# A two-block transformer kernel on one core: two row norms merged, the context normalised in the layer's tail, and a loop of two layers written out

## The chip, the cores and the metric

The kernel runs on one core of one Trainium2 chip. The metric is the device time of one execution, in microseconds. The kernel before took 1733.14 us, the median of three runs (1732.53 to 1736.98).

## The reference

Two blocks run one after the other on x, 256 tokens of 1024 values. The first is two hybrid attention layers, each `x + merged(x) @ w_out`, and a norm over each token's 1024 values. The second block takes the result and a context `ctx` of 256 tokens. Its first step is again a norm of both, followed by a gain, a scale and a shift.

```python
def rms_norm(x, gain):
    y = x * lax.rsqrt(jnp.mean(x * x, axis=-1, keepdims=True) + RMS_EPS)
    return y * gain

def first_block(...):
    for layer in range(DEPTH):                 # DEPTH = 2
        h = hybrid_layer(h, norm_gain[layer], w_in[layer], ..., w_out[layer])
    return rms_norm(h, final_gain)

def modulate(x, g, shift, scale):
    return rms_norm_2(x, g) * (1 + scale) + shift

def second_block(x, c, ctx, ...):
    # layer 0: even mixer, layer 1: attention, each followed by a convolved feed-forward
    h = modulate(x, norm1_g[0], sh1, sc1)
    h_c = modulate(ctx, norm1_g[0], csh1, csc1)
    ... even_mixer(h), even_mixer(h_c): p = h @ w_in; parts f, u, v of p ...
```

## The kernel before

All tensors are held transposed, 1024 values as KC = 8 chunks of 128 partitions with the tokens along the free dimension; `x_t` is x and `c_t` the context. A product is done in three matmuls on split operands: `w_hi` is the weight rounded to fp32r by ScalarE (`high(u)`, L1242 in the layers and L1398 behind them), `w_lo` the rest, by VectorE (`low(u)`, L1753 and L2025). The activations are split in the same way (`o_hi`/`o_lo`, `h2_hi`/`h2_lo`).

A unit is one load of 1 MB of weights into one of four slots of `raw` and the matmuls on them, into one or two of the three banks `banks_g` (a job each). `high` and `low` of a unit run two units ahead (AHEAD = 2), and SP loads a slot when the unit four before is done. A layer is the list `ORDER` of 48 units with what lies between them; `ada` entries are 24 small products for the second block's scales and shifts, each with a load of 1 MB of its own. Every engine walks the same list and emits its part of each entry; so the order on an engine is the order of the list, and semaphores counted by name (`Steps`) tie the engines together. Before the change each engine runs the layer as a hardware loop, `Fori(0, DEPTH)`, and values that depend on the layer sit in registers.

The layer's tail is units 44 to 47 (`out` 0 to 3). VectorE adds each product to `x_t` (L1812). ScalarE then rounds x times the next gain into `o_hi` (L1300, "x gain") and squares it into `qk[0]` (L1203), and VectorE makes `o_lo` (`x_low`, L1713) and adds the squares (L1708). In units 46 and 47 `high(0)`, `high(1)` and `first_low(0)`, `first_low(1)` (L1720) split the weights of the next pass, or of the units `vs` behind the last pass; `first_low` stands ahead of the addition of that unit's product. The layer ends with `ada turn` 1 on TensorE (L818), `mod now` on VectorE (L2004) and its copy to `mod` (L2017).

Behind the layers the list `END` sets the order. It begins with the final norm: sums of the squares over the partitions by matmuls with a column of ones (L712), a square root on ScalarE (L1519), a reciprocal (L2127), a spread of the 256 values over all partitions by a matmul (L1065) and eight multiplications into `x_t` (L2133). Then come transposes of the context (L1044), copies to `c_t` (L1497), squares of x and context (L1512), their additions (L2121), sums (L1059), root, spread (L1065) and the modulated norm in eight chunks: `h2` on VectorE for chunks 0 and 1 (L2142) and on GpSimd for the others (L1692), scale and shift on ScalarE (L1538), a cast and a subtraction on VectorE (L2149, L2152). Units `vs` 0 and 1 (L996 and L1020), of four 128-token tiles each, take these chunks; `sgu weights` transposes w_s (L1072), and unit `f` follows (L1032). `c_in` (the context as loaded) is issued on SP behind the last load of the layer (L657), and four constants are issued from ScalarE's queue (L1402 to L1405).

Of the kernel before, what the change touches and what calls it, by code (L numbers as in the profile page):

```python
# [50 lines left out]
SUM_COL = 352  # L51
# [60 lines left out]
class Steps:  # L112
# [13 lines left out]
    def step(self, *names):  # L126
        self.count[self.part] += 1
        for name in names:
            self.names[(self.part, name)] = self.count[self.part]
        return 1  # L130

# [61 lines left out]
def layer_order():  # L193
# [8 lines left out]
    for n, (kind, i) in enumerate(layer_units()):  # L202
# [39 lines left out]
        if n >= 44:  # L242
# [3 lines left out]
            order.append(("sums", n - 44))  # L246
        if n == 47:
            order.append(("ada turn", 1))
# [19 lines left out]
def end_order():  # L268

    order = [("final norm",), ("ctx",)]  # L270

    def all_squares(tag):
        order.extend(("squares", tag, c) for c in range(KC))
        order.extend(("sums", tag, c) for c in range(KC))
# [24 lines left out]
    all_squares("00")  # L299
    order.append(("mod norm", 0, 0))  # L300
    units("vs", 2)
# [45 lines left out]
END_UNITS = [(kind, i) for what, *rest in END if what == "unit" for kind, i in [rest]]  # L347
# [8 lines left out]
for _kind, _i in END_UNITS:  # L356
    for _j in range(end_jobs(_kind)):
        END_JOBS[(_kind, _i, _j)] = len(END_JOBS)
# [19 lines left out]
def program(nc, ins, out, known):  # L378
    with ExitStack() as ctx:
# [74 lines left out]
        add_parts = sb("add_parts", [P, 2 * PACK])  # L454
        token_rstd1 = sb("token_rstd1", [P, 2])
# [12 lines left out]
        s_cols = sb("s_cols", [P, KC, S_AT + 32])  # L468
# [54 lines left out]
        c_in = sb("c_in", [P, 2, D], offset=probs_at)  # L523
        used2 = max(used2, area + 16384 + 256)
        assert used2 <= SBUF_BYTES, used2
# [21 lines left out]
        end_loaded = sem("end_loaded")  # L547
        odd_loaded = sem("odd_loaded")
# [30 lines left out]
        def norm_tiles(tag):  # L579

            return 2 if tag in ("f", "11") else 4
# [23 lines left out]
        def _(sp):  # L605
# [4 lines left out]
            with sp.Fori(0, DEPTH) as layer:  # L610
                enter("layer", layer)
                w_in_l = ins["w_in"][bass.ds(layer, 1)].rearrange("l (c p) n -> (l p) c n", p=P)
# [5 lines left out]
                for u, (kind, i) in enumerate(UNITS):  # L618
# [5 lines left out]
                    if kind == "branch":  # L624
                        n, half = divmod(i, 2)
                        src = ins["w_branch"][bass.ds(layer, 1), n].rearrange("l (c p) n -> (l p) c n", p=P)[
                            :, :, half * 512:half * 512 + 512]
                        dst = slot.rearrange("p (c n) -> p c n", c=4)
                    else:
                        dst = slot.rearrange("p (c n) -> p c n", c=KC)  # L630
                        if kind == "out":
                            src = ins["w_out"][bass.ds(layer, 1)].rearrange("l (c p) n -> (l p) c n", p=P)[
# [8 lines left out]
                    sp.dma_start(dst, src).then_inc(raw_loaded[u % SLOTS], 16)  # L641
                    if u == 1:
# [3 lines left out]
                    if u and u % 2 == 0 or u == len(UNITS) - 1:  # L646
# [5 lines left out]
                                     ins["ada_w"][bass.ds(layer, 1)].rearrange("l (c p) n -> (l p) c n", p=P)[  # L652
# [3 lines left out]
            sp.wait_ge(pe_steps, pe_.at("values15"))  # L656
# [1618 lines left out]
```

## Time and profile before

| | |
|---|---|
| median of three runs | 1733.14 us |
| profiled execution, its own time | 1733.48 us |
| its span | 1731.7 us |
| PE busy / weight loads | 1637.4 us (95%) / 1431.8 us (83%) |
| VectorE (DVE) busy | 994.4 us (57%) |
| ScalarE (ACT) busy | 734.1 us (42%) |
| GpSimd (POOL) busy | 97.1 us (6%) |
| mean granted clock of TensorE | 0.971 |
| read from HBM | 256.67 MB |

PE is TensorE. Its matmuls overlap in the records, so that busy time is not time at its peak, and the distance between the starts of two matmuls tells more than their length. A granted clock of 1.0 is 2.4 GHz and one of 0.5 is 1.2 GHz. In a row of the timeline, the time in square brackets is how long the engine had been idle, and behind the arrow stands what ended it; a wait for several things is put down to the one that came last.

### The profile page before, as it was taken

How to read it: one execution, taken by the hardware profiler on the slowest of the kernel's cores; microseconds unless marked ns; L12 is line 12 of the kernel's file. 1: busy time of each engine (PE TensorE's matmuls, PEld its weight loads, DVE VectorE, ACT ScalarE, POOL GpSimd, SP SyncE). 2: the span in 40 equal slices, each digit the busy share in tenths (PEclk: the TensorE clock that was granted, in tenths of full speed). 3: DMA queues.
4: the chain of work that ended last, by engine and by line, in shares of the span. 5: the costliest groups of instructions: out<-in, count | busy, mean ns of one | idle time of the engine just before them, and what ended most of it. 6: DMA issues, size and time to landing. Idle time of an engine off the chain costs nothing.

```text
span 1731.7 us, 29254 instructions
## 1 busy us (share of the span) xinstructions
PE 1637.4 (95%) x11791; PEld 1431.8 (83%) x11791; DVE 994.4 (57%) x1243; ACT 734.1 (42%) x1072; POOL 97.1 (6%) x71
## 2 busy tenths in 40 slices
PE   6999999999999999779989999999979999989998
PEld 6998998989989989668777888888868785789998
DVE  6888566568885665563346433444344315677674
ACT  4545544445545444353235322233234233755453
POOL 0110000002100000020002000000011101210000
PEclk9999999999999999879999999999988998999999
DMA  7775665766766667602032223322233422145764
GB/s 253 232 251 175 219 218 192 249 209 215 244 197 217 195 196 240 220 25 98 25 97 70 85 67 108 115 86 78 87 110 101 125 73 61 38 147 172 206 180 125
DMA packets 329967, 259.68 MB, mean 150 GB/s; under 512 B 24017, under 2 KB 322385, under 8 KB 329826
## 3 DMA queue, kind: packets, MB, share of 16 engines
q1 hardware_dynamic: 311184, 251.55, 45.7%
q10 hardware_dynamic: 18642, 6.19, 1.7%
q8 instruction: 96, 1.57, 0.4%
q14 instruction: 45, 0.37, 0.1%
HBM read 256.67 MB, written 1.05 MB: 149 GB/s over the span
## 4 chain that ended last, share of the span: by engine, by line
PE 73%; DVE 14%; ACT 7%; issue 3%; DMA 2%; POOL 1%; ACTq 0%; SPq 0%; DVEq 0%
PE banks_g L1032 33%; PE banks_g L779 18%; PE banks_g L769 4%; PE banks_g L1020 3%; DVE w_lo L2025 3%; ACT w_hi L1398 3%; PE banks_g L802 2%; DVE w_lo L1753 2%; ACT w_hi L1242 1%; DVE conv L2074 1%; PE bank_s L899 1%; PE bank_t L912 1%; POOL h L1692 1%; DMA raw<-w_in 1%; DVE h_lo L2152 1%
## 5 line engine op out<-in xcount | busy, mean ns | idle before, releaser
L1032 PE MATMUL banks_g<-h_hi,w_lo 128*128 128x512 f32 (+1 forms) x864 | 297.7, 345 | 9.7 <-DVE h_lo L2152 9.7
L2025 DVE TENSOR_TENSOR w_lo<-raw,w_hi 128x2048 fp32r<-128x2048 f32 (+1 forms) x100 | 208.0, 2080 | 156.4 <-ACT w_hi L1398 156.4
L1032 PE MATMUL banks_g<-h_lo,w_hi 128*128 128x512 f32 (+1 forms) x864 | 295.8, 342 | 0.0
L1032 PE MATMUL banks_g<-h_hi,w_hi 128*128 128x512 f32 (+1 forms) x864 | 295.7, 342 | 0.0
L1753 DVE TENSOR_TENSOR w_lo<-raw,w_hi 128x2048 fp32r<-128x2048 f32 x92 | 210.7, 2290 | 82.1 <-ACT w_hi L1242 81.8
L779 PE MATMUL banks_g<-h_hi,w_lo 128*128 128x256 f32 x800 | 228.0, 285 | 0.0
L779 PE MATMUL banks_g<-h_lo,w_hi 128*128 128x256 f32 x800 | 223.4, 279 | 0.0
L779 PE MATMUL banks_g<-h_hi,w_hi 128*128 128x256 f32 x800 | 223.4, 279 | 0.0
L1398 ACT ACTIVATE w_hi<-raw 128x2048 fp32r<-128x2048 f32 (+1 forms) x100 | 173.3, 1735 | 73.6 <-DMA raw<-w_down 47.1
L1032 PEld LDWEIGHTS banks_g<-h_hi,w_lo 128*128 128x128 f32 x864 | 164.0, 190 | 33.3 <-DVE h_lo L2152 12.0
L1242 ACT ACTIVATE w_hi<-raw 128x2048 fp32r<-128x2048 f32 x96 | 182.9, 1905 | 7.4 <-DMA raw<-even_in 3.5
L1032 PEld LDWEIGHTS banks_g<-h_hi,w_hi 128*128 128x128 f32 x864 | 164.3, 190 | 21.0
L1032 PEld LDWEIGHTS banks_g<-h_lo,w_hi 128*128 128x128 f32 x864 | 164.3, 190 | 20.9
L1032 PE MATMUL banks_g<-f_hi,w_lo 128*128 128x512 f32 (+1 forms) x480 | 161.9, 337 | 3.0 <-DVE f_lo L2043 1.5
L1032 PE MATMUL banks_g<-f_hi,w_hi 128*128 128x512 f32 (+1 forms) x480 | 161.5, 336 | 0.0
L1032 PE MATMUL banks_g<-f_lo,w_hi 128*128 128x512 f32 (+1 forms) x480 | 161.5, 336 | 0.0
L779 PEld LDWEIGHTS banks_g<-h_hi,w_lo 128*128 128x128 f32 x800 | 151.1, 189 | 8.3 <-issue 5.0
L779 PEld LDWEIGHTS banks_g<-h_hi,w_hi 128*128 128x128 f32 x800 | 150.9, 189 | 0.0
L779 PEld LDWEIGHTS banks_g<-h_lo,w_hi 128*128 128x128 f32 x800 | 150.7, 188 | 0.0
L779 PE MATMUL banks_g<-o_hi,w_lo 128*128 128x256 f32 x480 | 135.4, 282 | 0.0
L779 PE MATMUL banks_g<-o_lo,w_hi 128*128 128x256 f32 x480 | 133.3, 278 | 0.0
L779 PE MATMUL banks_g<-o_hi,w_hi 128*128 128x256 f32 x480 | 133.3, 278 | 0.0
(322 smaller groups left out, 2882.8 us busy)
## 6 DMA issues: line engine op xcount, KB each, us to landing
raw<-w_in SPq DMA_DIRECT2D x76, 1024.0 KB, 5.1
ada_raw<-ada_w SPq DMA_DIRECT2D x48, 1024.0 KB, 7.3
raw<-w_up SPq DMA_DIRECT2D x88, 512.0 KB, 4.6
raw<-w_down SPq DMA_DIRECT2D x32, 704.0 KB, 4.4
raw<-w_branch SPq DMA_DIRECT2D x12, 1024.0 KB, 5.1
raw<-qkv SPq DMA_DIRECT2D x12, 1024.0 KB, 4.9
raw<-w_out SPq DMA_DIRECT2D x8, 1024.0 KB, 5.0
raw<-even_in SPq DMA_DIRECT2D x6, 1024.0 KB, 5.4
```

Source lines behind the costliest of these rows:

```text
L769: last = nc.tensor.matmul(ov[:, t, :], a[:, c, t * P:t * P + P], w[:, c, :], start=c == 0 and n == 0, stop=c == KC - 1 and n == 2)
L779: last = nc.tensor.matmul(ov[:, m, :], w[:, c, m0:m0 + P], a[:, a0 + c, :], start=c == 0 and n == 0, stop=c == kcs - 1 and n == 2)
L802: last = nc.tensor.matmul(gb[r, 0:256], s_cols[:, c, s0:s0 + 32], aw[:, c, :], start=c < 4, stop=c >= 4)
L899: last = nc.tensor.matmul(bank_s[:, 2 * e + j, 0:nk], qs[r, c, qt * P:qt * P + P], keys, start=x != "c", stop=True)
L912: last = nc.tensor.transpose(bank_t[:, s, :], probs[k % 2][:, s, kt * P:kt * P + P], ident[:, :])
L1020: last = nc.tensor.matmul(gb[:, tt * 256:tt * 256 + 256], a[:, c, t0:t0 + P], w[:, c, :], start=c == 0 and n == 0, stop=c == KC - 1 and n ...
L1032: last = nc.tensor.matmul(gb[:, m * SEQ:m * SEQ + nt], w[:, c, m0:m0 + P], a[:, c, 0:nt], start=c == 0 and n == 0, stop=c == kcs - 1 and n ...
L1242: nc.scalar.activation(w_hi[:, u % SLOTS, :], raw[:, u % SLOTS, :], ACT.Copy).then_inc(act_steps, act_.step(f"hi{u}"))
L1398: nc.scalar.activation(w_hi[:, u % SLOTS, 0:n], raw[:, u % SLOTS, 0:n], ACT.Copy).then_inc(act_steps, act_.step(f"hi{u}"))
L1692: nc.gpsimd.tensor_tensor(h2[:, c, t], x_streams[s_][:, c, :], m_rstd[:, t], ALU.mult).then_inc(pool_steps, pool_.step(f"normed{tag} {c}"))
L1753: nc.vector.tensor_tensor(w_lo[:, u % SLOTS, :], raw[:, u % SLOTS, :], w_hi[:, u % SLOTS, :].bitcast(F32), ALU.subtract).then_inc(dve_step ...
L2025: nc.vector.tensor_tensor(w_lo[:, u % SLOTS, 0:n], raw[:, u % SLOTS, 0:n], w_hi[:, u % SLOTS, 0:n].bitcast(F32), ALU.subtract).then_inc(dv ...
```

## The change

The two passes of the layer are written out for every engine: `Fori` becomes a Python loop, and `again()` sets the count of the steps back for each pass. `first_low(0)` and `first_low(1)` on VectorE, and `high(0)` and `high(1)` on ScalarE, move behind the additions and squares of units 46 and 47. The sums of the squares at the layer's start go to `bank_o` and no longer wait for `mod now`; the product `small` does.

In the second pass alone: SP issues the context and the four constants behind the weights of unit 42. The tail makes squares of x (qk[0]) and of x times the final gain (`y_sq`), no `o_hi` and no `o_lo`. "ctx prep" squares the rows of the context as loaded, with the sum along the row (tokens on partitions), takes their root and reciprocal, and scales the rows into `c_n`.

Behind the layers, the context comes first: `c_n` is transposed, gets gain and shift (ctx h), is split, and feeds the context half of `vs` 0. Both norms of x are got from one set of sums: r1 = 1/sqrt(sum x²/D + eps), r2 = 1/sqrt(r1² · sum (x·gain)²/D + eps); r1 and r1·r2 are spread together. h2 of x is one multiplication by both gains (`fg_gain`) and r1·r2; the shift goes into the rounding, and no work is left for GpSimd in this norm. `vs` is taken in four parts: 0 context, 1 context, 0 x, 1 x. The copies of the context into `c_t` and the final norm of `x_t` itself ("x prime") stand behind them. The diff, cut to its core:

```diff
@@ def end_order()
-    order = [("final norm",), ("ctx",)]
+    order = [("ctx turn", b) for b in range(4)] + [("final sums",)]
+    order += [("ctx h", 0), ("ctx h", 1), ("ctx split", 0), ("ctx h", 2), ("final root",), ("ctx h", 3), ("ctx split", 1),
+              ("second root",), ("ctx h", 4), ("ctx h", 5), ("ctx split", 2), ("ctx h", 6), ("ctx h", 7),
+              ("ctx split", 3)]
...
-    all_squares("00")
-    order.append(("mod norm", 0, 0))
-    units("vs", 2)
+    order += [("part", "vs", 0, 1), ("spread00",), ("x norm", 0)]
+    for c in range(1, KC):
+        order += [("x norm", c), ("x split", c - 1)]
+    order += [("x split", KC - 1), ("part", "vs", 1, 1), ("part", "vs", 0, 0), ("ahead", 2), ("part", "vs", 1, 0),
+              ("ahead", 3), ("ctx",), ("x prime",)]
@@ each engine
-            with pe.Fori(0, DEPTH) as layer:
+            for layer in range(DEPTH):
                 enter("layer", layer)
+                pe_.again()
@@ SP, in the layer
+                    if u == 42 and layer == DEPTH - 1:
+                        sp.dma_start(c_in[:, :, :], ins["ctx"][0].rearrange("(t p) f -> p t f", p=P)
+                                     ).then_inc(ctx_loaded, 16)
+                        sp.dma_start(dft_c[:, :], ins["dft_c"]).then_inc(end_loaded, 16)
+                        sp.dma_start(dft_t[:, :, :, :], ins["dft_t"]).then_inc(end_loaded, 16)
...
@@ ACT, in the layer
-                        high((u + AHEAD) % len(UNITS))
+                        if u + AHEAD < len(UNITS):
+                            high(u + AHEAD)
...
                         squares(i)
+                        if i >= 2:
+                            high(i - 2)
...
+                    elif what == "ctx prep" and layer == DEPTH - 1:
...
+                            for t in range(2):
+                                nc.scalar.activation(c_n[:, t, :], c_in[:, t, :], ACT.Square,
+                                                     accum_out=token_root[:, 2 + t:3 + t]).then_inc(ctx_ready, 1)
...
+                            nc.scalar.activation(c_n[:, t, :], c_in[:, t, :], ACT.Copy,
+                                                 scale=token_rstd[:, 2 + t:3 + t]).then_inc(ctx_ready, 1)
@@ DVE, in the layer
                         if u + AHEAD < len(UNITS):
                             low(u + AHEAD)
-                        else:
-                            first_low(u + AHEAD - len(UNITS))
...
+                        if i >= 2:
+                            first_low(i - 2)
@@ PE, behind the layers
+                elif what == "final sums":
+                    pe.wait_ge(dve_steps, dve_.at("gated15", before=True))
+                    pe.wait_ge(x_squared, 10)
+                    pe.wait_ge(act_steps, act_.at("squares3", before=True))
+                    for n, parts in ((2, [y_sq[:, a, j, :] for a in range(2) for j in range(2)]),
+                                     (0, [qk[0][:, j, :] for j in (0, 1, 6, 7)])):
+                        for t in range(2):
+                            for j in range(4):
+                                last = nc.tensor.matmul(bank_o[:, SUM_COL + n + t:SUM_COL + n + t + 1],
+                                                        parts[j][:, t * P:t * P + P], ones[:, 0:1],
+                                                        start=j == 0, stop=j == 3)
...
                 elif what == "ctx":
                     pe.wait_ge(ctx_loaded, 16)
+                    pe.wait_ge(act_steps, act_.at(f"ctx h{KC - 1}"))
@@ DVE, behind the layers
+                elif what == "ctx split":
+                    b, = arg
+                    if b == 0:
+                        dve.wait_ge(pe_steps, pe_.at("final sums"))
...
+                elif what == "x norm":
...
+                    nc.vector.scalar_tensor_tensor(h2[:, c, 0:SEQ], x_t[:, c, :], fg_gain[:, c:c + 1],
+                                                   bank_m[:, SEQ:2 * SEQ], ALU.mult, ALU.mult
+                                                   ).then_inc(dve_steps, dve_.step(f"x norm{c}"))
+                elif what == "x split":
...
+                    nc.vector.scalar_tensor_tensor(h2_lo[:, c, 0:SEQ], h2[:, c, 0:SEQ],
+                                                   mod[:, 0, mod_col(0) + c, 0:1], h2_hi[:, c, 0:SEQ].bitcast(F32),
+                                                   ALU.add, ALU.subtract).then_inc(dve_steps, dve_.step(f"x split{c}"))
```

## Rows read from the trace of the kernel before

**Rows 1.** The page: shares of the chain, and the two weight splits (busy, mean ns).
```profile
PE 73%; DVE 14%; ACT 7%; issue 3%; DMA 2%; POOL 1%; ACTq 0%; SPq 0%; DVEq 0%
...
L1753 DVE TENSOR_TENSOR w_lo<-raw,w_hi 128x2048 fp32r<-128x2048 f32 x92 | 210.7, 2290 | 82.1 <-ACT w_hi L1242 81.8
...
L1242 ACT ACTIVATE w_hi<-raw 128x2048 fp32r<-128x2048 f32 x96 | 182.9, 1905 | 7.4 <-DMA raw<-even_in 3.5
```

**Rows 2.** Windows: length, busy of PE, PEld, DVE, ACT, POOL; clock; DMA share; GB/s.
```profile
367.60:721.60 354.00, 342.75 (x3126) 315.70 (x3126) 248.59 (x319) 166.09 (x252) 17.45 (x6) 0.99 0.66 216
721.60:728.60 7.00, 0.00 (x0) 0.00 (x0) 5.28 (x7) 3.11 (x4) 0.00 (x0) 0.71 0.43 150
728.60:754.10 25.50, 10.07 (x44) 9.40 (x45) 11.32 (x25) 11.52 (x28) 0.77 (x1) 0.57 0.12 37
```

**Rows 3.** PE's waits, 300 to 782 us: total, times, longest.
```profile
PE bank_m L1059 <- DVE h L2121: 7.7, 1, 7.7
PE bank_m L712 <- DVE mod_now L2004: 7.1, 1, 7.1
```

**Rows 4.** The chain in order of time: start, us, what.
```profile
371.15 8.23 PE banks_g L761 x48
...
769.50 11.31 PE banks_g L1020 x96
...
781.24 22.42 PE banks_g L1032 x96
```

**Rows 5.** Timeline of PE at both layers' ends: start, us, instruction, idle before.
```profile
371.15 0.58 PE L761 MATMUL banks_g<-o_hi,w_lo 128*128 128x256 f32 x1 [3.56 <-DVE x_t L1812]
...
721.07 0.52 PE L818 MATMUL bank_m<-add_parts,ada_sum 128*128 128x24 f32 x4
```

**Rows 6.** Timeline of DVE between the layers.
```profile
370.35 0.68 DVE L1812 TENSOR_TENSOR x_t<-banks_g,x_t 128x512 f32<-128x512 f32 x1
...
376.74 0.17 DVE L1759 COPY gain<-vec 128x8 f32 x1 [2.95 <-issue]
```

**Rows 7.** Timeline of DVE at the end of the second layer.
```profile
723.31 2.29 DVE L1720 TENSOR_TENSOR w_lo<-raw,w_hi 128x2048 fp32r<-128x2048 f32 x1 [1.01 <-ACT w_hi L1242]
```

**Rows 8.** Timelines of DVE and ACT: durations of operations that the change reuses.
```profile
720.59 0.88 DVE L1713 SCALAR_TENSOR_TENSOR o_lo<-x_t,gain_next,o_hi 128x256 fp32r<-128x256 f32 x2
...
735.67 3.22 DVE L2133 SCALAR_TENSOR_TENSOR x_t<-x_t,vec,bank_m 128x256 f32<-128x256 f32 x8 [1.32 <-PE bank_m L1065]
...
752.80 0.43 DVE L2149 CAST h_hi<-h 128x512 fp32r<-128x512 f32 x1 [0.50 <-ACT h L1538]
753.26 0.69 DVE L2152 TENSOR_TENSOR h_lo<-h,h_hi 128x512 fp32r<-128x512 f32 x1
...
732.59 1.28 ACT L1519 ACT_TABLE_LOAD   x1 [4.93 <-issue]
```

**Rows 9.** Timelines of SP and PE in the second layer; landings of c_in and ada_raw.
```profile
664.11 0.37 SPq L641 DMA_DIRECT2D raw<-w_branch  x1
...
676.31 1.07 PE L802 MATMUL banks_g<-ada_raw,s_cols 128*32 128x256 f32 x16
...
714.50 1.07 PE L802 MATMUL banks_g<-ada_raw,s_cols 128*32 128x256 f32 x16
...
DMA to landing us min/median/max: 7.2/7.2/7.2
...
DMA to landing us min/median/max: 5.1/7.9/7.9
```

**Rows 10.** Timeline of PE: the sums of squares at either level of the clock.
```profile
380.31 1.05 PE L712 MATMUL bank_m<-ones,qk 128*128 128x1 f32 x8
...
728.65 1.87 PE L712 MATMUL bank_m<-ones,qk 128*128 128x1 f32 x8 [7.06 <-DVE mod_now L2004]
```

**Rows 11.** DMA view, instruction packets: 17 to 368 us, then 368 to 722 us.
```profile
q8 instruction: 25, 0.41, 0.4%
...
q8 instruction: 27, 0.44, 0.5%
```

More of the change, by code:

```diff
@@ L50 @@
 ADA_COL = 256
-SUM_COL = 352
+SUM_COL = 384
 ADA_UNITS = 24
@@ L130, in step, with again @@
         return 1
+    def again(self):
+        self.count["layer"] = 0
     def total(self, part):
@@ L246, in layer_order @@
             order.append(("sums", n - 44))
+        if 43 <= n <= 46:
+            order.append(("ctx prep", n - 43))
         if n == 47:
@@ L346 @@
 END = end_order()
-END_UNITS = [(kind, i) for what, *rest in END if what == "unit" for kind, i in [rest]]
+END_UNITS = list(dict.fromkeys((rest[0], rest[1]) for what, *rest in END if what in ("unit", "part")))
+END_U = {name: u for u, name in enumerate(END_UNITS)}
 def end_jobs(kind):
@@ L355 @@
 END_JOBS = {}
-for _kind, _i in END_UNITS:
-    for _j in range(end_jobs(_kind)):
-        END_JOBS[(_kind, _i, _j)] = len(END_JOBS)
+for _what, *_rest in END:
+    if _what == "unit":
+        for _j in range(end_jobs(_rest[0])):
+            END_JOBS[(*_rest, _j)] = len(END_JOBS)
+    elif _what == "part":
+        END_JOBS[tuple(_rest)] = len(END_JOBS)
 END_JOB_AT = {n: job for job, n in END_JOBS.items()}
@@ L703, in _, with sum_squares @@
                 last.then_inc(pe_steps, pe_.step(f"x turned{b}"))
[L705 to L709 removed]
+            def sum_squares(layer):
+                pe.wait_ge(dve_steps, dve_.at("gated15", before=True))
+                pe.wait_ge(x_squared, layer * 3 + 3)
                 for t in range(2):
                     for j in range(2):
[L712 removed]
+                        last = nc.tensor.matmul(bank_o[:, SUM_COL + t:SUM_COL + t + 1],
                                                 qk[0][:, j, t * P:t * P + P], ones[:, 0:1],
@@ L833, in _ @@
                     elif what == "small":
-                        pe.wait_ge(act_steps, act_.at("root"))
                         pe.wait_ge(dve_steps, dve_.at("small lo"))
+                        pe.wait_ge(dve_steps, dve_.at("mod now", before=True))
                         n = 0
@@ L1230, in _ @@
                                      ).then_inc(act_steps, act_.step("s cols"))
-            with act.Fori(0, DEPTH) as layer:
+            for layer in range(DEPTH):
                 enter("layer", layer)
+                act_.again()
                 def high(u):
@@ L1650, in _ @@
             pool.wait_ge(consts_loaded, 16 * CONSTS)
-            with pool.Fori(0, DEPTH) as layer:
+            for layer in range(DEPTH):
                 enter("layer", layer)
+                pool_.again()
                 before = "rope r"
@@ L1744, in _ @@
             dve.wait_ge(consts_loaded, 16 * CONSTS)
-            with dve.Fori(0, DEPTH) as layer:
+            for layer in range(DEPTH):
                 enter("layer", layer)
+                dve_.again()
                 def low(u):
@@ L2016, in _ @@
                 own()
-                nc.vector.tensor_copy(mod[:, bass.ds(layer, 1), :, :], mod_now[:, :, :]
+                nc.vector.tensor_copy(mod[:, layer:layer + 1, :, :], mod_now[:, :, :]
                                       ).then_inc(dve_steps, dve_.step("mod"))
@@ L2122, in _ @@
                             dve_steps, dve_.step(f"added{tag} {c}"))
-                elif what in ("final norm", "mod norm"):
-                    tag = "f" if what == "final norm" else f"{arg[0]}{arg[1]}"
+                elif what == "mod norm":
+                    tag = f"{arg[0]}{arg[1]}"
                     tiles = norm_tiles(tag)
```

331 lines of the change are left out of this document (216 added, 115 removed).

## Prediction

> **What bounds the kernel now.** I began with the page: the chain of work that ended last is 73% PE, and a split of one 2048-wide weight unit costs 1.9 us on ACT and then 2.29 on DVE [rows 1]. A change counts for what it takes out of PE's waits. The windows come next [rows 2]: in the second layer PE is busy for 342.75 of 354.00 us; in the 32.5 us from 721.6 to 754.1 it is busy for 10.07 us in all, at a granted clock of 0.57 to 0.71, and that on sums, spreads and transposes only. The list of waits names the holes in that stretch [rows 3]: 7.1 us for mod_now, which stands in DVE's queue behind the last w_lo split (L1720, from 723.31) and the last addition to x (about 725.5, though its product was ready at 721.07) [rows 7], and 7.7 us for the additions of the squares. The chain gives the pace and the end of the stretch [rows 4]: 96 matmuls in 11.31 us, 0.118 us each, and unit f starts at 781.24. The layer's last matmuls (L818, 721.07 and 0.52 long [rows 5]) end at 721.6. Between the two lie 59.6 us that hold 192 matmuls of vs, 22.6 us at that pace. So some 37 us are at stake, less what the norms really need.
>
> A second hole lies between the layers: PE starts unit 0 at 371.15 after 3.56 us of idle time [rows 5], so it was free at 367.6. The granted clock is at its lower level, 1.2 GHz, after these 3.56 us without work, and the 48 matmuls take 8.23 us [rows 4] in place of 48 x 0.118 = 5.65.
>
> **Part 1, between the layers.** Two edits meet here: the loops are written out, and first_low (2.29 us) moves behind the additions to x. What ends the 3.56 us is ambiguous: the row names x_t (L1812, 370.35 to 371.03), which stood behind a first_low; but DVE itself has 2.95 us of "issue" idle before the first instruction of the next pass [rows 6], where nothing keeps it waiting, so the jump back costs time of its own. Both are removed. The new order: unit 47 and ada 23 (1.07 [rows 9]) take PE's last 6.7 us, so the product of unit 46 is there at 360.4 and is now added at once; hi(0) follows squares(2) on ACT and ends at about 364.6, first_low(0) at 366.9, before PE is free at 367.6. The last addition runs 367.1 to 367.8, x hi 6 and 7 to 368.7, x_low (0.44 each [rows 8]) to 369.3; unit 0 needs them for its last 12 matmuls, from 371.8. High(1) ends at 371.2, first_low(1) at 373.5; unit 1 comes behind unit 0 (367.6 + 5.65 = 373.2), ada 0 and sumsq (1.07 and 1.05), at 375.3. No wait is left and the clock stays up. Unit 0 ends at 373.2 for 379.4: **6.2 us** saved, 3.6 of the gap and 2.6 of the clock. The ends: 0 if PE must pay a fetch there in a straight run too; the same 6.2 if only x_t was late.
>
> Of fetching, the DMA view shows 25 packets of instructions during the first pass and 27 during the second [rows 11]: the second pass is fetched again already, and written out it fetches nothing more. The Trainium skill (Runtime: NRT & Kernel Launch, Instruction fetch mechanics) says that prefetch is purely sequential and that a taken branch out of the resident pages stalls; DVE's 2.95 us agree with it.
>
> **Part 2, the loads moved into the layer.** SP issues ctx (1 MB) and four constants (0.9 MB) behind unit 42's weights, at 664.11. Queued behind them on SP and on the DMA engines: ada 20, then the weights of units 43 and 44. An ada alone lands 5.1 us after its issue; c_in, 0.6 us behind another, took 7.2 and an ada just behind unit weights 7.9 [rows 9]: each further MB adds 2.7 to 3.8 us. So unit 42 lands at 669.2, the 1.9 MB at about 674.6, ada 20 at 677.4 to 678.3; PE wants ada 20 at 676.31. I take **+1.5 us** (0 to +3). The weights of 43 land at about 681, their split takes 4.2 us, and unit 43 is wanted about two units of PE behind ada 20: hidden. In return four issues in ACT's queue ahead of the final root go; that is inside part 4's new order.
>
> **Part 3, the tail of the second layer.** Added to ACT: two squares and two scaled copies of 128x1024, 1.0 each (half of 1.9), a table load of 1.28 [rows 8], a root of 0.3; to DVE three operations of 0.2 and two additions of 0.69. The x hi copies become squares, x_low goes. Behind them on ACT stand the weight splits: high(46) ends at 702.8 for 700.9; high(47) at 710.9, behind the root; low(47) at 713.2, needed by unit 47 at 715.5 (ada 23 at 714.50 and 1.07 [rows 9]). Behind low(47) on DVE, the addition that frees out1's bank ends at 713.9, also needed at 715.5. So all is hidden, with 1.6 us to spare. The Trainium skill (ScalarE: Activation LUTs, What ACT_TABLE_LOAD costs) adds a drain of 1.38 us to a load; this trace shows the root 0.02 us behind the load. By the page the slack would shrink to 0.2 us and the sum stay.
>
> Then out2's addition ends 717.6, x hi 718.5, squares 719.1, high(0) 721.0, the last context copy 722.0; first_low(0) 723.3, out3's addition 724.0, its squares 725.5, high(1) 727.4, first_low(1) 729.7, mod 730.3.
>
> **Part 4, behind the layer.** PE: twelve context transposes from 722.1, four more at 724.0, from 725.5 the final sums, 16 matmuls of one column where there were 4. Four took 1.05 us at 2.4 GHz and 1.87 at 1.2 [rows 10]: 16 are 4.2 or 7.5 us. Before, the clock was down at 728.65, after 7 us idle; here PE works 1.8 of 4 us. I take the lower level, since such light work did not raise it before either (0.57 from 728.6 to 754.1 [rows 2]): sums to 733.0, other end 729.7. [...]
>
> DVE's first context split waits for the sums: cast 0.43, subtraction 0.69 [rows 8], their forms without POOL at work: 734.2; the small steps of the root 734.9; splits 1 to 3, with r12 between them, 736.0, 737.6, 738.8. PE takes the first 48 matmuls (vs 0, context) from 734.2, with the clock down at first, as unit 0 did: 8.2 us, 742.4, longer than the splits. Spread, 4 matmuls: 743.5. Then vs 1, context, 5.65: 749.1. Beside it x is made: product 0.40 [rows 8], split 0.45, some 0.87 a chunk, from 743.9 to 751.3. PE takes up x at 749.1, 0.71 a chunk, chunk 7 at 754.1: no wait. vs 0 ends 754.8, vs 1 760.4, sixteen transposes 762.3.
>
> **The new wait:** on ACT stand, in this order, the gelu of the last vs (761.0), high(3) 1.9 (762.9) and only then four 128x512 copies of c_t, 0.5 each (764.9); the transposes of w_s wait for the last. PE idles 2.6 us, and f starts at 765.6. Behind that, x prime (8 x 0.40, after low(3), to 768.4) holds low(4) to 770.7, needed two units on: hidden. Saved up to f: 781.24 - 765.6 = **15.6 us**.
>
> **Sum**, against the profiled execution's own 1733.48 us (1.8 above its span; the median is 1733.14): 1733.5 - 6.2 + 1.5 - 15.6 = 1713.2. Behind f order, loads and bound are the old ones.
>
> **Rivals.**
> - The clock stays up through the sums: PE's gaps there are short. They end 3.3 us earlier: 1709.9; if it stays up into vs too, 2.6 more, 1707.3. Chance 0.20.
> - More waits: the pause before f drops the clock too (2.6 us, as unit 0 paid), or ada 20 and out1's bank come later: 1716. Chance 0.17.
> - Part 1 doesn't do what it says, PE pays a fetch there anyway: 1713.2 + 6.2 = 1719.4. Against: no wait of that size on "issue" among PE's [rows 3]. Chance 0.09.
> - Slower than before: written out, PE's stream outruns its fetch when the DMA engines are loaded (share 0.66 in the layer [rows 2]). A miss priced like the 3.56 us gap must come six times to eat 20 us; ten of the 27 fetches would give 1713.2 + 35.6 = 1748.8. Against: the end part is straight already and its PE shows none. Chance 0.02.
> - Within 0.3%: parts 1 and 4 both lose most of their gain (order kept, clock down to f): about 1730. Chance 0.02.
>
> **How the numbers follow.** Forecast 0.50, at 1713.2. The 80% range takes in the bounds of ada 20 (-1.5, +1.5) and the cases beside it, and leaves out the failure of part 1: 1707 to 1719. The bound for same, 0.3% or 5.2 us, is about what a measurement of this kernel can tell from no change: faster 0.96, same 0.02, slower 0.02.
>
> **What would show it.** PE's gap between the layers gone and unit 0 at 5.65 us; ada 20 waited for by 1 to 2 us; final sums of some 7 us; unit f about 20 us earlier; a new PE wait of 2 to 3 us for c_t ahead of it. It is wrong if PE waits for the splits of x, if low(47) or out1's bank stalls PE before 721, or if stages behind f change length.

## Result and the profile after

The changed kernel takes 1723.05 us (median of six runs, 1716.71 to 1725.65) beside 1734.45 for the kernel before: ratio 0.9929, 95% interval 0.9911 to 0.9947. It is faster by 11.4 us where 20 were forecast; 1723 lies 4 us above the top of the range. A second measurement, beside later experiments, gave 1721.12 and 0.9922 (0.9908 to 0.9936). The profiled executions, 1719.86 against 1733.48, are 13.6 us apart, and the account below is made between those two; the one of the changed kernel is the second fastest of its six.

The windows of PE in the kernel after come first (length, busy time of PE, PEld, DVE, ACT and POOL with their counts, granted clock, DMA share, GB/s). The last one runs from the end of the layer's last product to the start of unit f:

```profile
0.00:369.90 369.90, 347.19 (x3146) 319.77 (x3147) 256.71 (x332) 174.81 (x266) 19.18 (x15) 0.99 0.68 224
369.90:724.40 354.50, 343.57 (x3143) 315.93 (x3143) 248.05 (x320) 174.23 (x263) 18.40 (x6) 1.00 0.67 220
720.70:762.40 41.70, 36.08 (x270) 35.34 (x270) 21.13 (x37) 20.72 (x34) 0.00 (x0) 0.88 0.22 77
```

The same stretch in the kernel before, which holds the two last windows of [rows 2] and the matmuls of vs behind them:

```profile
721.60:781.24 59.64, 36.33 (x241) 34.94 (x242) 33.57 (x48) 28.30 (x51) 12.01 (x12) 0.74 0.16 51
```

PE is busy for 36 us in both; the stretch has shrunk from 59.6 to 41.7 us. The two long waits of [rows 3] are gone. What PE waits for in the whole run now (total, times, longest):

```profile
PE bank_t L941 <- DVE probs L1887: 13.9, 10, 2.3
PE bank_t L1137 <- DVE token_rstd L2304: 5.7, 3, 1.9
PE bank_t L1144 <- ACT c_t L1613: 2.8, 1, 2.8
...
PE banks_g L832 <- DMA ada_raw<-ada_w: 0.8, 1, 0.8
```

and what answered to the first two in the kernel before:

```profile
PE bank_t L912 <- DVE probs L1775: 11.2, 10, 1.7
PE bank_t L1065 <- DVE token_rstd L2127: 2.3, 4, 0.6
```

Ten waits for probs have grown by 2.7 us in all, though the attention of the layers is not among the things that the change names; and three waits for token_rstd cost 5.7 us where four cost 2.3.

Where the time went shows best in the same piece of PE's work in both traces, each timed from its own first instruction. The shift is the start after less the start before (negative is earlier), at anchors that both kernels have:

| place in PE's stream | start before | start after | shift |
|---|---|---|---|
| first unit | 17.36 | 17.43 | +0.1 |
| an ada product late in layer 0 | 334.41 | 336.57 | +2.2 |
| ada 0 of layer 1, behind unit 0 | 379.31 | 375.59 | -3.7 |
| last probs of layer 1 | 643.66 | 641.95 | -1.7 |
| ada 22 of layer 1 | 702.00 | 701.13 | -0.9 |
| transposes of w_s, just ahead of unit f | 780.64 | 761.75 | -18.9 |
| spread of the norm "01" | 905.25 | 887.73 | -17.5 |
| spread of the norm "10" | 1288.29 | 1272.99 | -15.3 |
| first up unit of the last FFN | 1539.77 | 1525.68 | -14.1 |
| last down units | 1633.04 | 1619.63 | -13.4 |

So the boundary gave 5.9 and the tail 18.0; the layers took 2.1 and 2.9 back, and the stages behind unit f took 5.5 (each is the difference of two shifts, before rounding). The chain of the kernel after through the tail, in order of time (start, length, what), shows no long piece in which PE idles:

```profile
724.42 5.00 PE bank_o L1024 x32
...
729.44 0.44 DVE h_hi L2192
...
729.90 0.69 DVE h_lo L2194
730.60 0.09 DVE token_r L2199
...
730.74 8.62 PE banks_g L999 x48
739.36 0.89 PE bank_m L1034 x8
740.25 16.98 PE banks_g L999 x144
...
757.28 0.47 issue
757.75 1.90 ACT w_hi L1497
759.65 1.96 ACT c_t L1613 x4
...
761.75 0.63 PE bank_t L1144 x4
```

Three things stand in it: the sums take 5.0 us, unit vs 0's context half is slow (8.6, as unit 0 once was in [rows 4]) and the other 144 matmuls of vs run at full pace without a gap, and then ACT's split of 1.90 stands ahead of the copies of c_t.

### The profile page after: what moved, and what is told of

Read it like the earlier page. It is cut to its first block, busy times and chain, and to the rows that moved or that the text cites. A ratio compares the mean times of both kernels' runs of the same rounds, so it can differ in the third digit from the quotient of the medians.

```text
span 1718.0 us, 27660 instructions
## 1 busy us (share of the span) xinstructions
PE 1637.9 (95%) x11819; PEld 1431.4 (83%) x11819; DVE 980.7 (57%) x1238; ACT 731.2 (43%) x1062; POOL 86.6 (5%) x59
## 4 chain that ended last, share of the span: by engine, by line
PE 55%; DVE 12%; ACT 6%; issue 2%; DMA 1%; POOL 1%; SPq 0%; DVEq 0%; ACTq 0%
PE banks_g L1109 33%; PE banks_g L809 6%; DVE w_lo L2154 3%; PE banks_g L1097 3%; ACT w_hi L1497 3%; DVE w_lo L1865 2%; PE banks_g L999 1%; DVE conv L2252 1%; ACT w_hi L1315 1%; POOL h L1803 1%; PE bank_t L1165 1%; PE banks_g L1079 1%; PE banks_g L799 1%; PE banks_g L832 1%; PE bank_m L1189 1%
```

## Experiments

Every ratio is to the kernel before, on the same chip, with its 95% interval. Two questions were open: what the layers pay, and what the norms behind x prime pay. A third was which of two edits closed the gap between the layers.

### The boundary: jump or order

One kernel writes the loops out and leaves the order:

```diff
-            with dve.Fori(0, DEPTH) as layer:
+            for layer in range(DEPTH):
+                dve_.again()
```

(and so for the other four engines). 

> The kernel before with its five loops over the layers written out and nothing else changed. Theory A: writing out costs each layer 2 to 3 us (waits that were register compares become instructions of their own on DVE's chains: PE's waits for probs at 2.3, 2.0, 0.9 and 1.8 us for 1.7, 1.6, 0.5 and 1.3). At the boundary between the layers, if the jump was the cause, the gap of 3.56 us goes and the clock stays up (6.2 us gained): net about -1 us against before. If x_t, late behind first_low, was the cause, the gap stays above 3 us and the net is +4 to +5. Rival B, the prediction's: the layers cost nothing by being written out and only the boundary changes: -3 to -6 us. Rival C, a straight stream is fetched late: the layers grow with waits on issue, not with longer waits for probs.

The other keeps the loops and moves only the splits:

```diff
 (ACT, squares i)
+                        if i >= 2:
+                            high(i - 2)
 (DVE, sums i)
+                        if i >= 2:
+                            first_low(i - 2)
```

(and takes them out of units 46 and 47, as the change does).

> The kernel before with its loops kept; only the first two weight splits of the next layer (high 0 and 1 on ACT, first_low 0 and 1 on DVE) are moved behind the squares and sums of out3, as the change has them. If x_t late behind first_low made the 3.56 us gap between the layers, the gap goes: -6 us against before, and the tail of the second layer is untouched. If the jump back made it (DVE showed 2.95 us of issue there), some 3 us of gap stay, the clock still falls, and the time is within 1 us of before. Both layers should keep their old lengths otherwise (waits for probs 1.7, 1.6, 0.5, 1.3).

Measured: loops written out 1733.09, ratio 0.9989 (0.9977 to 1.0); order alone 1734.71, ratio 0.9989 (0.9979 to 1.0). Timelines of PE at the start of unit 0, first the loops written out, with the row ahead of it, then the order alone:

```profile
370.94 0.52 PE L823 MATMUL bank_m<-add_parts,ada_sum 128*128 128x24 f32 x4
371.30 0.36 PE L766 MATMUL banks_g<-o_hi,w_lo 128*128 128x256 f32 x1
```

```profile
371.98 0.58 PE L761 MATMUL banks_g<-o_hi,w_lo 128*128 128x256 f32 x1 [4.42 <-issue]
```

Written out, PE goes on without a gap although first_low still stands where it stood. With the order alone the gap is as long as ever (4.42) and the row now says what it is: issue, PE's own jump back. The name x_t in [rows 5] was that of the last thing that happened to end in the jump's shadow. DVE pays its own jump too, in the kernel with the order alone 2.94 us as in [rows 6]:

```profile
376.94 0.17 DVE L1762 COPY gain<-vec 128x8 f32 x1 [2.94 <-issue]
```

and in the kernel after nothing between the same instructions:

```profile
376.04 0.21 DVE L2146 COPY mod<-mod_now 128x96 f32<-128x96 f32 x1
376.29 0.17 DVE L1871 COPY gain<-vec 128x8 f32<-128x8 f32 x1
```

The Trainium skill (Runtime: NRT & Kernel Launch, Instruction fetch mechanics) says that a taken branch whose target is not in the resident pages stalls the engine; the 4.42 us on issue agree with it. The second half of the result was theory A's: writing the loops out brought 6.0 us at the boundary (shift +3.9 ahead of it, -2.2 behind unit 0), and the profiled run was 1.8 us slower than the kernel before all the same. The waits for probs had become those of the changed kernel, 15.1 us for 11.2. By the times alone (1.9 us faster, 0 to 4.0) theory A and rival B can't be told apart; by the waits they can. So the layers' loss belongs to the loops written out, not to the tail's new work. Rival C is out: no new wait on issue stands among PE's.

### What the layers pay: which wait the instruction carries

Between the two traces one piece of DVE's chain in layer 0 differs. Timelines of DVE, before and after:

```profile
127.04 0.42 DVE L1996 TENSOR_TENSOR ada_sum<-ada_sum,banks_g 128x256 f32<-128x256 f32 x1
127.50 0.69 DVE L1929 SCALAR_TENSOR_TENSOR probs<-bank_s,causal 128x512 f32<-128x512 f32 x1
```

```profile
128.19 0.42 DVE L2125 TENSOR_TENSOR ada_sum<-ada_sum,banks_g 128x256 f32<-128x256 f32 x1 [0.46 <-DVE g L1927]
128.72 0.69 DVE L2058 SCALAR_TENSOR_TENSOR probs<-bank_s,causal 128x512 f32<-128x512 f32 x1
```

From the start of ada_sum to that of probs it is 0.46 us before and 0.53 after. The idle 0.46 us ahead of ada_sum belongs to the same difference: it stands in all seven kernels with the loops written out and the waits in their old order, and in none of the other seven (in the loop with the pairs turned round, shown below, it is missing too). PE's product had been ready since 125.09 there, and DVE's own last result since 127.74. Why this step pays 0.4 us and most others 0.07 is open. The groups of lines show the same step where it recurs: o_lo behind ACT's o_hi, twelve times in layer 0 (the last number is the idle time ahead of them), before and after:

```profile
L1982 DVE TENSOR_TENSOR o_lo<-o_gated,o_hi 128x256 fp32r<-128x256 f32 x12 | 5.1, 425 | 5.8 <-ACT o_hi L1375 5.8
```

```profile
L2111 DVE TENSOR_TENSOR o_lo<-o_gated,o_hi 128x256 fp32r<-128x256 f32 x12 | 5.1, 426 | 6.6 <-ACT o_hi L1476 6.6
```

0.8 us in twelve, 0.07 each. These instructions wait for two things: another engine's result, and DVE's own last one (`own()`). In the traces an instruction that computes carries at most one wait; the other stands in an instruction of its own. DVE has 277 semaphore instructions before, plus 818 register operations that work out the loop's values, and 491 and none after. Which wait stands where, as the records have it (99 is PE's semaphore, 101 DVE's own):

```
before  register operation waits for 99, probs carries 101
after   semaphore instruction waits for 101, probs carries 99
```

In the loop the instruction carries the wait that is listed last, in straight code the one listed first. For probs the wait that ends last is DVE's own, for the ada_sum just ahead of it; for o_lo, where `own()` is listed first, it is ACT's o_hi. So the change turned these pairs round, without a word of them in its diff: in either case the wait that ends last has become the separate instruction. The test is to turn them back, in the layer's DVE steps alone:

```diff
+                            own()
                             dve.wait_ge(pe_steps, pe_.at(f"scores{k}"))
-                            own()
```

(In the same way for values, exp, job and ada; at o_lo the wait for o_hi goes ahead of `own()`, and at the gates the one for tanh ahead of the one for the job.) 

> The changed kernel with one thing altered: where a DVE instruction of a layer has two waits, they are listed in the other order, so that the one that ends last is the one carried by the instruction and the one long met is the separate instruction. Theory: the 2.3 and 2.9 us that each layer lost come from that separate instruction standing behind the wait that ends last (about 0.07 us on each step of the dependent chain). Then the waits for probs fall back to about 1.7, 1.6, 0.5 and 1.3 us and the kernel is 3 to 5 us faster than the changed one. Rival, the lost time comes from the fetch of straight code or from the order of loads: nothing changes (within 1 us). The norms behind x prime keep their 1.9 us waits in either case.

Measured: 1716.84, ratio 0.9889 (0.9875 to 0.9903), against 0.9929 and 0.9922. DVE's timeline and the group of o_lo have their old values again, and PE waits 11.4 us for probs for 13.9:

```profile
126.77 0.42 DVE L2127 TENSOR_TENSOR ada_sum<-ada_sum,banks_g 128x256 f32<-128x256 f32 x1
127.23 0.69 DVE L2059 SCALAR_TENSOR_TENSOR probs<-bank_s,causal 128x512 f32<-128x512 f32 x1
```

```profile
L2112 DVE TENSOR_TENSOR o_lo<-o_gated,o_hi 128x256 fp32r<-128x256 f32 x12 | 5.1, 425 | 5.8 <-ACT o_hi L1476 5.8
```

```profile
PE bank_t L941 <- DVE probs L1887: 11.4, 10, 1.7
```

Against the changed kernel PE's shift grows by 2.2 us through layer 0 and by 2.5 through layer 1 (some 1 us of it a stretch at the lower clock that the changed kernel has at 501 us and this one has not). The code is as straight and as long as before, so fetch is no cause of it. The other profiles say the same: by PE's shift against the kernel before, each layer costs at most 0.5 us in the four kernels with the pairs turned back, and 1.6 to 4.0 us (layer 0) and 2.5 to 5.0 us (layer 1) in the seven others that are written out.

The profiled execution of this run shows a second thing. It took 1720.76, no less than the changed kernel's, for it lost its lead again: 1.5 us behind the wait for c_t, where the clock fell, 0.8 at the norm "01", and 3.4 in the last down units. There PE's matmuls start 0.118 us apart where they start 0.113 apart in the changed kernel and in the kernel before, at a granted clock of 1.00 in all (680 matmuls against 702 between 1620 and 1700 us). Both paces occur in every trace; what sets them no run here shows, and it is part of the scatter of all these times.

Without the rest of the change: loops written out, waits in the new order. 

> The kernel before with its loops written out and the layer's DVE waits listed in the new order, nothing else. Theory: writing out brings 6 us at the boundary and costs some 3 us a layer only through the separate wait instructions; with the order mended the cost goes and the boundary's gain is left: 5 to 7 us below the kernel before, waits for probs at 11.3 us in all for 15.1. Rival (the layers' loss is the fetch of straight code): it stays where the loops alone were, 0 to 2 us below before.

Measured: 1728.06, ratio 0.9967 (0.9954 to 0.998), 6.0 us below before; waits for probs 10.0 in all. Timeline of PE at the boundary:

```profile
367.42 0.52 PE L823 MATMUL bank_m<-add_parts,ada_sum 128*128 128x24 f32 x4
367.79 0.37 PE L766 MATMUL banks_g<-o_hi,w_lo 128*128 128x256 f32 x1
```

This is the boundary's 6 us by itself, and it needs no moved splits: first_low stands where it stood.

The last one is the same reordering in the kernel before, loops kept. 

> The kernel before, loops kept, with the layer's DVE waits listed in the new order and nothing else. Theory: in a loop the waits compare with a register that is worked out ahead, and the kernel before already had the short waits (probs 11.2 us in all); what the listing can still save is little: 0 to 2 us below the kernel before. Rival: the order of the waits is worth its 5 us in any code, loop or straight, and the changed kernel's loss in the layers is something else: then 4 us or more below before.

Measured: 1741.69, ratio 1.0044 (1.0029 to 1.0059), slower by 7.6 us. Both expectations missed, and the miss says most. I had taken waits in a loop to be indifferent, since registers are worked out ahead. They are not: in the kernel before, the pairs only happened to be the right way round. Turned round, the loop pays what the changed kernel pays: waits for probs from 11.2 to 14.4, the distance from ada_sum to probs 0.54 (127.89 to 128.43), the idle time ahead of o_lo 6.9 for 5.8.

```profile
PE bank_t L912 <- DVE probs L1775: 14.4, 10, 2.0
```

So the cost follows neither the loop nor the straight code, but whether the wait that ends last is an instruction of its own. The same edit is worth -5 us in one and +7.6 in the other. The Trainium skill (Perfetto Trace Analysis, Per-engine timelines) draws the wait of a DVE or ACT instruction in a queue that it is pushed to after decoding, and that of a sequencer-only instruction in the sequencer, which fetches the next one only behind it. If a semaphore instruction is of the second kind, what follows it is decoded after the wait has ended; the 0.07 us a step would fit that, but no run here measures the decoding itself.

### What the norms pay: a table load behind a wait

The diff puts a wait for mod (met since 729 us) ahead of ACT's wait for the sums of the squares, in the three norms behind x prime. Timelines of ACT at the norm "01", before, then after:

```profile
902.76 1.28 ACT L1519 ACT_TABLE_LOAD   x1
904.72 0.26 ACT L1519 ACTIVATE token_root<-bank_m,eps 128x4 f32<-128x4 f32 x1 [0.68 <-PE bank_m L1059]
```

```profile
885.90 1.28 ACT L1631 ACT_TABLE_LOAD   x1 [2.02 <-PE bank_m L1132]
887.20 0.26 ACT L1631 ACTIVATE token_root<-bank_m,eps 128x4 f32<-128x4 f32 x1
```

Before, the table was loaded while ACT had nothing to do, and the root came 0.68 us later, when PE's sums ended. After, PE's sums are waited for by a semaphore instruction (885.86), the load comes behind it, and the root carries the wait for mod; so the load's 1.28 us stand on the path. One run leaves the wait out:

```diff
-                    act.wait_ge(dve_steps, dve_.at("mod", before=True))
                     act.wait_ge(pe_steps, pe_.at(f"sumsq{tag}"))
```

> The changed kernel without the one wait that the change put ahead of ACT's wait for the squares in the three norms behind x prime. Theory: of two waits ahead of an instruction one becomes an instruction of its own, and the table load for the root comes only behind it, so its 1.28 us stands on the path of each of the three norms (PE's waits for token_rstd went from 0.57 to 1.91, 0.57 to 1.91 and 0.55 to 1.89). Then these three waits are back at about 0.57 and the kernel is 3 x 1.34 = 4.0 us faster than the changed one, 1719.0 for 1723.05. Rival: the waits grew for a reason that comes from further ahead (the stages arrive in another order of DMA and clock); then they stay at 1.9 and the time stays within 1 us.

Measured: 1715.47, ratio 0.9876 (0.986 to 0.9893). The other keeps both waits and changes places:

```diff
-                    act.wait_ge(dve_steps, dve_.at("mod", before=True))
                     act.wait_ge(pe_steps, pe_.at(f"sumsq{tag}"))
+                    act.wait_ge(dve_steps, dve_.at("mod", before=True))
```

> The changed kernel with both waits of the three later norms kept, but the one for the squares' sums listed ahead of the one for mod. Theory: in straight code the instruction carries the wait that is listed first and the other one becomes an instruction of its own; the one for mod was met long ago, so the table load runs while ACT still waits for the sums, and PE's waits for token_rstd are back at about 0.57 each: 4 us below the changed kernel, as without the wait. Rival: any second wait puts the table load behind the wait for the sums; then 1.9 us each and no gain.

Measured: 1713.7, ratio 0.9888 (0.9863 to 0.9913). The separate instruction is now the wait for mod (884.55), and the root carries the one for the sums. Its ACT timeline, and its row among PE's waits, which in the run without the wait reads 1.7, 3, 0.6 as well:

```profile
885.28 1.28 ACT L1631 ACT_TABLE_LOAD   x1
887.24 0.26 ACT L1631 ACTIVATE token_root<-bank_m,eps 128x4 f32<-128x4 f32 x1 [0.68 <-PE bank_m L1132]
```

```profile
PE bank_t L1137 <- DVE token_rstd L2304: 1.7, 3, 0.6
```

4.0 us of PE's waiting go in both, whether the wait for mod is left out or only listed second. The times fell by 5 to 9 us against the changed kernel's 1721 to 1723; the intervals are 3 to 4 us wide, and the 4.0 us of the waits are what the traces bear out. Of the named rivals this run leaves none: both waits are still there, and the load runs early again.

### The tail: what the order brings, and the wait for c_t

PE multiplies x ahead of the context, all else as in the change:

```diff
-    order += [("part", "vs", 0, 1), ("spread00",), ("x norm", 0)]
+    order += [("spread00",), ("x norm", 0)]
...
-    order += [("x split", KC - 1), ("part", "vs", 1, 1), ("part", "vs", 0, 0), ("ahead", 2), ("part", "vs", 1, 0),
+    order += [("x split", KC - 1), ("part", "vs", 0, 0), ("part", "vs", 1, 0), ("part", "vs", 0, 1), ("ahead", 2), ("part", "vs", 1, 1),
```

(and each part's own waits with it.) 

> The changed kernel with PE's order in the first two units behind the layer turned back: x is multiplied ahead of the context, with everything else as in the change. Theory: the context's 48 matmuls cover the chain root, spread, product and split of x (730.7 to 739.2 in the changed kernel); with x first PE idles from the sums (729.4) until split 0 of x at about 736, then four parts of 48 follow, 8.2 us and three of 5.65: vs ends at about 761 for 757.1. So 4 us slower than the changed kernel, up to 6 if the clock stays low for longer; most of the tail's 18 us stays, since it comes from the norms' work moved ahead. Rival: the order is what brings the gain, then 8 us or more are lost.

Measured: 1726.39, ratio 0.9955 (0.9942 to 0.9968). One of the six executions took 5630.45 us; the median of the others is 1724.80, 3.7 us slower than the changed kernel beside it (1721.12). PE's timeline has the two holes that the context covers in the changed kernel:

```profile
722.65 5.18 PE L1024 MATMUL bank_o<-ones,qk 128*128 128x1 f32 x32 [0.90 <-ACT qk L1275]
730.88 2.07 PE L1034 MATMUL bank_m<-ident,token_r 128*128 128x128 f32 x8 [3.04 <-DVE token_r L2210]
734.68 0.55 PE L999 MATMUL banks_g<-w_hi,h_lo 128*128 128x256 f32 x1 [1.73 <-DVE h_lo L2222]
```

From ada 22 to the transposes of w_s PE gains 14.4 us on the kernel before here, for 18.0 and 19.6 in the two profiles of the changed kernel. So 4 to 5 us of the tail's 18 come from multiplying the context first, as expected; the rest comes with the norms' work done ahead and at once, which no run takes apart further.

The copies of c_t ahead of the split of unit 3:

```diff
-              ("ahead", 3), ("ctx",), ("x prime",)]
+              ("ctx",), ("ahead", 3), ("x prime",)]
```

> The changed kernel with the four copies of c_t ahead of the weight split of unit 3 (high 3, 1.9 us) on ACT, nothing else. Theory: high 3 stands between the last gelu and the copies, PE waits for the last copy, so its wait falls from 2.8 to 0.9 us, f starts 1.9 us earlier, and nothing behind it needs the split of unit 3 sooner (the three edits together showed 1.8 there): 1.5 to 2 us below the changed kernel. Rival: unit f 0's or f 1's split comes late instead and PE waits for w_lo; then no gain.

Measured: 1715.45, ratio 0.9891 (0.9872 to 0.9911). PE's timeline of this kernel:

```profile
761.09 0.63 PE L1144 MATMUL bank_t<-ident,w_s 128*128 128x128 f32 x4 [0.99 <-ACT c_t L1613]
```

The wait falls from 2.78 to 0.99, and no wait for w_lo appears behind it: 1.8 us as expected. The time fell by more; in its profiled execution the rest came between 1270 and 1440 us, where the lower clock lasted less long, and no part of it can be put down to the edit.

### The changed kernel again, and a faster one

> The changed kernel once more, unaltered, beside the others on the same chip. Both theories: 11 to 14 us faster than the kernel before. The same waits must show up again if they belong to the program: PE for probs 2.3 and 2.0 us in each layer (13.9 us in all), three waits of 1.9 us for token_rstd, 2.8 us for c_t; what differs from the first profile is then chance (the clock's low stretches in the layers, 3.4 us at 501).

Measured: 1721.12, 13.0 us below the kernel before. All the waits named recur (token_rstd 5.7, c_t 2.8, probs 14.6); what does not recur are the places at which the clock falls. One of them matters: behind the pause for c_t the granted clock is at 0.50 from 762.2 to 765.6 here, which costs 1.5 us up to 800, and in the first profile it stayed up.

The wait for mod out, the waits in the new order, and c_t first, together: 

> The changed kernel with three edits: the wait for mod ahead of the three later norms is out, the waits of the layer's DVE steps are listed with the one that ends last at the instruction, and the four copies of c_t stand ahead of the split of unit 3's weights (high 3) on ACT. Theory: the causes are apart and add up: 4.0 for the norms, 5.3 for the layers (the shift that the wait order alone showed by 700 us), 1.9 for c_t (PE waits 0.9 us for 2.8): 10 to 11 us below the changed kernel, 21 to 24 below the kernel before, about 1711. Rival: what is gained is given back behind x prime, where loads or the clock set the pace; then no more than 6 us below the changed kernel.

Measured: 1704.29, ratio 0.9839 (0.9817 to 0.9861). And with the loads moved behind ada 20:

```diff
+                    if u and u % 2 == 0 or u == len(UNITS) - 1:
...
+                        sp.dma_start(ada_raw[:, :].rearrange("p (c n) -> p c n", c=KC),
...
                     if u == 42 and layer == DEPTH - 1:
...
-                    if u and u % 2 == 0 or u == len(UNITS) - 1:
...
-                        sp.dma_start(ada_raw[:, :].rearrange("p (c n) -> p c n", c=KC),
```

> The version with three edits and one more: the 1.9 MB of context and constants are issued behind ada 20, not ahead of it. Theory: PE's wait of 0.8 us for ada 20 in the changed kernel (1.5 us in two others) goes, the context lands some 3 us later than now and its squares on ACT still end in time; 0.5 to 1.5 us below the version with three edits. Rival: the context lands too late, the splits of unit 46 and 47 behind its squares on ACT come late, and PE waits in the layer's tail: 1 to 3 us slower.

Measured: 1703.4, ratio 0.9818 (0.9798 to 0.9837). PE's timelines at ada 20, with three edits and with the fourth:

```profile
670.53 1.07 PE L832 MATMUL banks_g<-ada_raw,s_cols 128*32 128x256 f32 x16 [0.71 <-DMA ada_raw<-ada_w]
```

```profile
669.69 1.07 PE L832 MATMUL banks_g<-ada_raw,s_cols 128*32 128x256 f32 x16
```

The wait of 0.71 is gone and no new one has come in the tail, but by their times the two versions can't be told apart. Both beat the changed kernel, by 17 to 18 us, and the kernel before by 30. The three edits were to bring 10 to 11; all three waits shrink as they do one by one, but the sum came out larger. Part of it is the clock, as far as the traces show: behind x prime the profiled run is at its lower level for less time (of PE's window from 721 to 765 us the mean granted clock is 0.92 for 0.88, and around each norm a shorter hole is followed by a shorter low stretch: the shift grows by 1.3 us at the wait of the norm "01" and by another 0.9 in the matmuls behind it). I did not test that apart.

## Why the prediction came out as it did

- **Boundary, -6.2 forecast, -5.9 measured.** Right in size. Of its two causes only one was real: the jump. Moving first_low was worth nothing there.
- **Ada 20, +1.5 forecast, +0.8 measured** (wait of 0.80 for its load). Right mechanism, a little large.
- **Work added to the layer's tail, hidden with 1.6 us to spare.** Right: no wait for low(47) nor for out1's bank.
- **Tail, -15.6 forecast, -18.0 measured.** The term that was mis-sized is the final sums: 7.5 us at the lower clock forecast, 4.99 measured, because the clock fell only in the middle of them, between 726.6 and 726.8 (the windows stand in the last section). The prediction had set the low level for all of them; the trace has 2.2 us of the sums at the full one. That is the first rival's side (4.2 us), come half true. Behind it the steps hold: vs 0's context half 8.5 us (8.2), no wait for any chunk of x, and the new wait of 2.78 for c_t (2.6). The pause did not lower the clock in this execution; in the second profile of the same kernel it did, by 1.5 us, which is the second rival's case.
- **"Behind f order, loads and bound are the old ones".** This sentence failed: -18.9 became -13.4. The diff has a new wait in these norms, for a semaphore that had long been met. The prediction prices the new waits for ada 20 and c_t and puts this one at nothing. It made the wait for the sums an instruction of its own, with the table load behind it: 3 x 1.34 = 4.0 us. The other 1.5 us are left over; the clock is at its lower level for 71.6 us behind unit f where it was for 61.3, which is a likely part of it, but no run isolates that.
- **The layers themselves, put at nothing but fetching.** This failed as well: the prediction has no term for waits inside the written-out layers. 2.1 and 2.9 us went there, 0.8 of them ada 20's, some 1 the stretch of lower clock at 501 us; the rest are pairs of waits turned round, as the kernels with the pairs turned back show. The rival that I set for slower code in the layers was fetching, at 0.02; no wait on issue stands among PE's, and turning the pairs back took the cost away with the code still written out.

From the sum: 1713.2 - 2.4 (tail) + 4.0 (norms) + 5.0 - 0.8 (layers without ada 20) - 0.7 (ada 20) + 0.3 (boundary) + 1.5 (left over behind f) is 1720.1, against the profiled 1719.86. It closes because its terms are read from the same two executions. That the profiled time lies only 1 us above the range is in part luck: the tail's surplus hid 2.4 us of the costs. The prediction's own sign of being wrong, stages behind f that change length, is the one that came. What the range lacked is a case for costs in stages that the sum does not touch.

## What to carry to other kernels

That an added wait has long been met does not make it free. Where an instruction has two waits, see in the trace which of them it carries: the one that ends last must be that one, and anything that could run early, a table load above all, must not come to stand behind it. Whether the first or the last listed is carried changed here with writing out a loop, so after such an edit compare the waits of the stages that it was not meant to touch. And where a wait ends together with a jump, keep the loop and move the supposed culprit: if the gap stays, it was the jump.

## What the runs showed of the hardware

- Jumping back cost PE 3.56 to 4.42 us of idle time and DVE 2.9; without the jump PE had no gap.
- A wait that ends last and stands as an instruction of its own cost 0.07 us on most steps of a dependent chain of DVE, and 0.4 us at some ada_sum in straight code (127.77 to 128.19); turning the pairs back was worth 4 to 6 us over both layers in the changed kernel, and turning them the wrong way cost the kernel before 7.6.
- The load of a table (1.28 us) runs ahead of the wait that its instruction carries, but not ahead of a wait that stands before it as an instruction; nothing further was seen between load and root (885.90 + 1.28, root at 887.20). The Trainium skill (ScalarE: Activation LUTs, What ACT_TABLE_LOAD costs) adds a drain of 1.38 us to the load; the trace has none here.
- PE's matmuls of 128x256 started 0.113 or 0.118 us apart at a granted clock of 1.00: from 1620 to 1700 us it was 702 of them in the kernel after and 680 in the run with the pairs turned back.
- The sums of one column began at 2.4 GHz, behind 4.2 us in which PE had worked for 2.7, on the layer's last product and on transposes, and went on at 1.2 GHz; in [rows 10], behind 7 us of idle time, they were at 1.2 GHz from the first. Windows of PE in the kernel after (length, busy, clock, DMA share, GB/s):

```profile
720.20:724.40 4.20, 2.71 (x22) 1.00 0.67 229
724.40:726.60 2.20, 2.18 (x20) 1.00 0.12 43
726.80:729.40 2.60, 2.60 (x13) 0.50 0.00 0
```
